# Up projections of a gated feed-forward by seven block products for eight, with the down projection in three groups

## What is computed

```
def conv_ffn(h, w_up, conv_w, conv_b, w_down):
    u = causal_dwconv(h @ w_up, conv_w) + conv_b
    gate, up = jnp.split(u, 2, axis=-1)
    return (jax.nn.silu(gate) * up) @ w_down
...
x = x + conv_ffn(rmsnorm(x, ffn_norm[layer]), ...)
```

## Time and profile before

| | |
|---|---|
| median of 3 runs | 2572.43 us (2566.87 to 2572.94) |
| the profiled execution | 2572.35 us, span of the core 2570.6 us |
| PE busy | 2326.0 us, 90% of the span |
| PEld, the weight loads (beside PE) | 1163.4 us, 45% |
| DVE, ACT, POOL busy | 1097.3, 692.2, 889.6 us (43, 27, 35%) |
| share of the chain that ended last, PE | 40% |
| granted PE clock, mean | 0.929 of full |

### The profile page before, as it was taken

How to read it: one execution, slowest core, us unless ns; L and a number is a source line. 1 busy time by engine, 2 the same in 40 slices (tenths; PEclk the granted TensorE clock), 3 DMA queues, 4 the chain that set the end, 5 groups by cost and what they waited for, 6 DMA issues and landing times. The chain is left out here.

```text
span 2570.6 us, 32294 instructions
## 1 busy us (share of the span) xinstructions
PE 2326.0 (90%) x12070; PEld 1163.4 (45%) x12070; DVE 1097.3 (43%) x1585; ACT 692.2 (27%) x989; POOL 889.6 (35%) x671
## 2 busy tenths in 40 slices
PE   5877657888999999999987989899899999999998
PEld 3433325644444444444443444885444444444444
DVE  7678888835433333321140043953453333331001
ACT  5245556612323222200021213311132222220000
POOL 6002304223434433444348022312343344334432
PEclk7888879999999999999998999558999999999999
DMA  4001100001111111111123001000111111111112
GB/s 148 17 1 33 39 11 1 18 25 41 50 49 49 49 53 53 47 54 45 53 61 98 0 26 33 9 1 17 49 34 56 49 49 49 50 56 45 51 53 80
DMA packets 185946, 109.32 MB, mean 43 GB/s; under 512 B 3871, under 2 KB 180422, under 8 KB 185878
## 3 DMA queue, kind: packets, MB, share of 16 engines
q1 hardware_dynamic: 185414, 107.00, 13.9%
q0 software_dynamic: 464, 1.39, 0.2%
HBM read 104.18 MB, written 4.19 MB: 42 GB/s over the span
## 5 line engine op out<-in xcount | busy, mean ns | idle before, releaser
L503 POOL TENSOR_SCALAR w_scaled<-stage 128x1024 f32<-128x1024 f32 (+1 forms) x184 | 189.7, 1031 | 1351.4 <-PE ps L699 1328.6
L699 PE MATMUL ps<-h_hi,w_hi 128*128 128x512 f16 x1696 | 511.1, 383 | 70.7 <-ACT work L1168 40.7
L699 PE MATMUL ps<-h_lo,w_hi 128*128 128x512 f16 x1696 | 510.3, 383 | 0.0
L699 PE MATMUL ps<-h_hi,w_lo 128*128 128x512 f16 x1696 | 509.8, 382 | 0.0
L699 PE MATMUL ps<-arena,w_hi 128*128 128x512 f16 x1920 | 494.9, 380 | 2.9 <-DVE small L1765 2.6
L1782 DVE SCALAR_TENSOR_TENSOR work<-ps,fvec,work 128x1023 f32<-128x1023 f32 (+1 forms) x176 | 225.5, 1282 | 509.0 <-ACT work L1233 496.1
L506 POOL TENSOR_TENSOR w_lo<-w_scaled,w_hi 128x1024 f16<-128x1024 f32 (+1 forms) x176 | 369.2, 2098 | 14.7
L699 PEld LDWEIGHTS ps<-arena,w_hi 128*128 128x128 f16 x1920 | 188.2, 98 | 231.6 <-issue 6.7
L699 PEld LDWEIGHTS ps<-h_hi,w_hi 128*128 128x128 f16 x1696 | 166.2, 99 | 276.9 <-issue 82.6
L699 PE MATMUL ps<-arena,w_lo 128*128 128x512 f16 x960 | 286.4, 380 | 0.0
L699 PEld LDWEIGHTS ps<-h_lo,w_hi 128*128 128x128 f16 x1696 | 167.5, 99 | 204.8 <-issue 8.0
(11 more groups left out here) (302 smaller groups left out, 2364.0 us busy)
## 6 DMA issues: line engine op xcount, KB each, us to landing
stage<-in_ffn_w_up_dram SPq DMA_DIRECT2D x88, 512.0 KB, 3.8
stage<-in_ffn_w_down_dram SPq DMA_DIRECT2D x32, 512.0 KB, 3.6
stage<-in_od_w_in_dram SPq DMA_DIRECT2D x20, 512.0 KB, 3.7
stage<-in_ev_w_in_dram SPq DMA_DIRECT2D x12, 512.0 KB, 3.6
stage<-in_ffn_w_down_dram SPq DMA_DIRECT2D x16, 384.0 KB, 3.2
arena<-in_x_dram SPq DMA_DIRECT2D x8, 512.0 KB, 6.3
stage<-in_ev_w_out_dram SPq DMA_DIRECT2D x8, 512.0 KB, 3.6
stage<-in_od_w_out_dram SPq DMA_DIRECT2D x8, 512.0 KB, 3.6
```

What stands on the lines that cost most here:

```text
L503: nc.gpsimd.tensor_scalar(scaled, src, W_SCALE, 1.0, ALU.mult, ALU.mult).then_inc(w_parts, 1)
L699: last = mm(out2[:, hf * HALF:(hf + 1) * HALF], w, a[:, k0 + k, hf * HALF:(hf + 1) * HALF], start=(first and k == 0 and pss == 0), stop=(l ...
```

## The change

In the 20 hidden tiles f = 2 to 21 of each layer, the gate and the up unit are computed together. The weights of the pair are seen as a 2x2 block matrix (gate and up by the two halves of the 1024 input channels), the activations as another (halves of the channels by halves of the positions). Eight block products of 12 matmuls make 96; here there are seven products, by sums of the weight blocks and of the activation blocks, and sums of the products: 84 matmuls.

- **POOL** no longer scales (L503) or rounds (L504) up weights. It makes four sums of 512-column blocks (`su_sums`) and the low parts of all seven blocks (`su_lows`), eight TENSOR_TENSOR instructions a pair.
- **ACT** scales both stage buffers in place (`su_scale`, 2048 elements), makes the high parts of seven blocks (`su_hi_raw`, `su_hi_sums`), and copies product P1 out of PSUM (`keep_p1`). The feed-forward on ACT, DVE and POOL is written out without loops.
- **DVE** makes four sums of activation blocks after the norm (2048 elements each), and five sums a pair (`cross`, 512 elements with one operand in PSUM) that PE and the convolution wait for.
- **PE** keeps the products of one f in four banks x, z, y, w, and waits inside a pair for DVE's sums: P7 for U2, P4 for U3, P3 for C22.
- **SP** loads both weight tiles of f+1 when POOL has read those of f (`su_read`): there is one `stage` for both, so a pair is not loaded while the one before it is still read.
- **f = 1** is computed plainly (96 matmuls), but from the new weight buffers, whose high part ACT makes ahead of its 16 norm tiles and whose low part POOL makes ahead of its norm tiles.
- **Memory.** The sums need room, so the hidden tiles are a ring of eight: groups of 8, 8 and 6 hidden tiles, each followed by its own down projection over all eight m, added to the residual: 24 residual additions a layer in place of 8. The first matmuls of a down projection wait for the last hidden tiles of the group.
- Outside the feed-forward, the **indexer** starts at block 2.

The core of the diff:

```diff
+            def su_sums(layer, f):
+                pool.wait_ge(su_scaled, X0 + su_of(layer, f) + 1)
...
+                if j:
+                    pool.wait_ge(su_split, j)
+                    pool.wait_ge(su_hi, hi_count(layer, f - 1) if f > 2 else hi_count(0, FT - 1))
+                G.tensor_tensor(sums_a[:, 0, :], up[:, 0, :], up[:, 1, :], ALU.add).then_inc(su_sum, 1)
+                G.tensor_tensor(sums_a[:, 1, :], gate[:, 0, :], up[:, 0, :], ALU.subtract).then_inc(su_sum, 1)
...
+            def ffn_split(layer):
+                split_section(f"up{layer}", 2, 1, peeled=2)
+                su_lows(layer, 1)
+                norm_lows(1 + 2 * layer)
+                su_sums(layer, 2)
+                su_lows(layer, 2)
+                for i, op in enumerate((1, 0, 2)):
+                    top_low(layer, i + 1, op)
+                su_sums(layer, 3)
+                top_low(layer, 4, 3)
+                su_lows(layer, 3)
+                for g, (f0, nf) in enumerate(GROUPS):
+                    for f in range(max(f0, 4), f0 + nf):
+                        su_sums(layer, f)
+                        su_lows(layer, f)
+                    pool.wait_ge(su_split, cross_of(layer, f0 + nf - 1) + 1)
+                    split_section(f"down{layer}{'abc'[g]}", 2, 4, lambda u: nf * P)
...
+                def crossed(f, i):
...
+                    pe.wait_ge(conv_done, i * 4 + (c0 + 2 * set_user(f) + 2))
...
+                    pe.wait_ge(su_split, i * 2 + (j + 1))
+                    product(x, A11, s, b_of(h_hi, 0, 0), b_of(h_lo, 0, 0), True)
...
+                    product(y, S2, s, *tops[1], True)
...
+                    product(z, S1, s, *tops[0], True)
...
+                    pe.wait_ge(cross_step, i * 10 + (5 * j + U2))
+                    product(y, S3, s, *tops[2], False)
+                    pe.wait_ge(p1_copied, i * 2 + (X0 + j + 1))
+                    product(x, A12, s, b_of(h_hi, 1, 0), b_of(h_lo, 1, 0), False)
...
+                    pe.wait_ge(cross_step, i * 10 + (5 * j + U3))
+                    product(y, A22, s, b_of(h_hi, 0, 1), b_of(h_lo, 0, 1), False)
+                    pe.wait_ge(cross_step, i * 10 + (5 * j + C22))
+                    product(z, S4, s, b_of(h_hi, 1, 1), b_of(h_lo, 1, 1), False)
...
+                if n % 2:
+                    su_scale(n // 2, 1)
+                    su_hi_raw(n // 2, 1)
                 for m in range(2 * KT):
                     hf, k = divmod(m, KT)
+                    if n % 2 and m == 12:
+                        su_scale(n // 2, 2)
...
+                    for f in range(max(f0, 2), f0 + nf):
+                        cross(f, U2)
+                        if f > f0:
+                            hidden(f - 1)
+                        cross(f, U3)
+                        cross(f, C22)
+                        if f > f0:
+                            hidden_low(f - 1)
+                        cross(f, C21)
+                        cross(f, C12)
+                        conv(f)
...
-            for b in range(NB):
+            for b in range(2, NB):
```

391 lines of the change are left out of this document (298 added, 93 removed).

## The result

The changed kernel takes 2529.85 us (median of 4 runs, 2521.63 to 2534.58); the kernel before, run beside it, 2569.65 (4 runs, 2566.8 to 2572.94). The ratio is 0.9844, 95% interval 0.9818 to 0.987: 1.6% faster, where 0.8% was forecast (2552). The sign was right, and the time lies in the range, at the number of rival A. The gain was twice the forecast.

What follows compares the result with a forecast made beforehand. PE, busy 90% of the span, was taken to bound the kernel. Removing 119.3 us and adding 49.1 a layer (98.2) gave net -21.1 from 2572.4, 2551.3, said as 2552 us; range 2528 to 2586.

Steps and rivals of the forecast that it cites:

- rival A: Feed-forward start mostly covered: costs 5 to 14 us for 20, short waits cost no clock; 2530 us; chance 0.13.
- Removed, 119.3 us: Time taken away: 103.6 us of matmuls, 12.1 of waits and low clock at the third unit, 3.6 of indexer blocks.
- The start: Start of each feed-forward: second norm tile 4.2 us later, then PE waits taken as 20 us, range 0 to 28.
- the walk: Start followed through POOL, ACT and DVE: POOL's lows of f = 3 ready at 709.8; PE stalls 18.5 us in all.
- The last stall: PE before P7 of f = 3: 2.6 us, as tap 2 of f = 2 stands on ACT behind a scale.
- ends of groups: Down projection's last k waits for the last hidden tile, 11.3 us after P3: 2.2 + 2.2 + 4.8 = 9.2 us a layer.
- Starts of groups: Next group's weights wait for the last down split: 4.5 us before P1, 0.6 before P7, twice a layer: 10.2 us.
- Clock behind these places: Clock falls after three waits a layer of 4.5 to 4.8 us: 3 x 2.05 less 0.6, 5.5 us.
- the clock behind waits of 2.2 to 2.9 us: PE's clock after these shorter waits: 0 to 2.8 us lost each, taken as 0.
- B: P7's wait for U2 in steady pairs: 0.6 us of room, sums come 1.0 later, 14 us lost; 2566 us; chance 0.15.
- C: The weight ring (load, scale, sums, lows) sets the steady pair's pace at 19.0 us, costing 31 us; 2583 us; chance 0.17.
- D: Clock falls inside the pairs, as PE waits on seven semaphores a pair: 72 us, 2624 us; chance 0.03.

Runs made afterwards that it cites:

- x_norm: Changed kernel with POOL making the first norm low part ahead of the weights' low parts of f = 1: 2533.48 us.
- x_nw: Changed kernel with matmuls without a use on PE in front of each feed-forward's norm, 80 small and 8 of 512 columns: 2527.63 us.
- x_pw: x_pre with 20 matmuls without a use on PE before P7 of f = 2: 2509.49 us.
- x_en: x_early with the edit of x_norm added: 2516.48 us.
- x_early: Changed kernel with the high parts of the weights' sums of f = 2 moved ahead on ACT, before an activation's high part and two tap 2: 2524.42 us.
- x_tops: Changed kernel with DVE's four activation sums at a layer's start cut to 16 columns of each block: 2517.24 us.
- x_pre: Changed kernel with the first pair's weights of the second and third group loaded, scaled and split ahead of the down weights: 2502.24 us, ratio 0.9747 to the kernel before.
- x_order: Changed kernel with DVE's hidden low part of tile 0 moved behind the subtraction U2 of f = 2: 2534.82 us.

## Why the gain was twice the forecast

Removed, 119.3 us: right but for the indexer. The 103.6 us of matmuls are confirmed by the 20.72 us pairs. Of the 3.6 us 0.8 was seen at the residual, inside a scatter of 3 us: **2.8 less** than forecast. Forecast for the feed-forwards alone was 115.7 - 98.2 = 17.5 us; measured 37.0. So what the change adds was put at 49.1 us a layer, and that was too much.

**The start was the failing step**: second tile 4.2 and waits 20, 24.2 us a layer. By my own walk PE without waits would have come to P7 of f = 3 at 697.5, 82.4 us after the residual (655.0, 675.8 and 693.9 of the walk, each less the 4.2, plus three products). It came 714.45 - 614.31 = 100.1 after it, in layer 1 98.9. **The start costs 17.8 and 16.5 us, not 24.2.** Of the low clock all that lies ahead of this is in it. In PE's rows 9.2 us of it are waits before L857 (7.0 in layer 1), where I had announced about 20, at three places and not six; the rest is mostly the second tile, 4.1 us later after the residual than before the change, and matmuls at the lower clock.

Adding the two terms was no double count, since the walk's waits are counted from a PE that is already 4.2 late. But they are not two costs that could be saved one by one. x_norm, x_nw and x_pw made PE earlier or faster ahead of P7 of f = 2, and it came 77.1 to 77.4 us after the residual, as in the changed kernel (77.2 and 77.0); x_en did so on top of x_early, and it stayed at x_early's 74.0. There is one cost, the lateness at the end of the chain, and that is what the walk had wrong.

**Where the walk was long.** It has POOL's lows of f = 3, for which PE waits at that tile's first product, ready at 709.8, 94.7 us after the residual. They ended at 704.0, 89.7 after it. Of these 5.0 us 2.0 lie ahead of POOL's last norm low (I had 649.8, it was 646.95): the 1.9 us for the scale of f = 2 cost nothing there. Behind it I had 60.0 us and it took 57.05. POOL's waits for ACT came to 5.1 us and not 9: the one for the sums' high parts was there, the one at the sums of f = 3 was not. The exclusions by DVE's four sums were 6.1 and not 8.5. Against that about 3.4 us came up that I had not counted, mostly POOL instructions that took 0.45 to 1.0 us longer beside other work of DVE.

The last stall, before P7 of f = 3, came as walked, from tap 2 behind a scale that waits for a load, in layer 0 2.37 us for 2.6 and in layer 1 0.65. Then I put 1.5 on top, from 18.5 to "I take 20", with bounds of 0 and 28: nothing but caution pointed up. So the wait of POOL for ACT is the main term that was mis-sized, 5.1 for 9, then the exclusion, 6.1 for 8.5, and by x_tops the chain hung not on what POOL lost by exclusion, but on DVE's first three sums and the 3.4 us for which POOL held them.

Smaller terms, a layer: ends of groups 1.44 + 1.44 + 4.02 = 6.9, forecast 9.2. From P3 the last hidden tile took 10.7 us and not 11.3 (the convolution 5.10 for 5.33, hand-overs the rest) and PE's cover was 9.2 and not 9.06, so the step was right and the size off by 0.8 at each. Starts of groups 8.1 and 8.7, forecast 10.2: the waits were 4.1 for 4.5, and the 0.6 before the next P7 did not come, as far as can be told because of the 1.2 us of room. Clock behind these places: 1.8 a start by x_pre, 1.5 and 2.5 at the last end (in windows of 2 us, busy time by what the clock lacked of 1.00): 5.1 and 6.1, forecast 5.5.

One term I had put at nothing, the clock behind waits of 2.2 to 2.9 us. In layer 0 four products follow P7 of f = 3 and its wait of 2.37 us without a pause, and take 12.1 us where in layer 1, behind 0.65 us, they take 10.3; the clock over them:

```profile
714.45:726.55 12.10, 12.10 (x49) 5.19 (x50) 5.90 (x5) 4.61 (x4) 9.49 (x7) 0.86 0.31 87
```

That is 1.7 us. At this place PE waited 2.1 to 2.6 us in twelve feed-forwards of the kernels with whole pairs of seven products, and behind nine of them the same 1.7 us are lost, behind three nothing. x_order's +3.0 us in layer 1 are for the most part this: its P7 of f = 3 comes 1.0 us later, after a wait of 2.3, and the four products behind it take 1.7 longer.

Added in all: 17.8 + 6.9 + 8.1 + 5.1 + 1.7 = 39.6 in layer 0, 16.5 + 6.9 + 8.7 + 6.1 = 38.2 in layer 1, for 49.1 each. The removed side is 51.8 us of matmuls a layer and the third unit's 5.3 and 6.8. That makes the feed-forwards 57.1 - 39.6 = 17.5 and 58.6 - 38.2 = 20.4 us shorter, measured 17.1 and 19.9.

**The rivals.** A gave 2530 for a start of 5 to 14 us, the second tile's 4.2 not counted; the time is A's, the reason is half so. In A's terms the start cost 13.6 and 12.3, at the upper end, and POOL's lost time did run into its wait for ACT, though DVE's sums lay on the chain. Short waits did lose clock, and 8.2 us of what I had put too high were at the ends and starts of groups. B and C named real limits with too little room given them: 1.2 us for B's 0.6, and a ring of 16.05 for C's 19.0. D: none; the window over four pairs shows 1.00. On the rule of the Trainium skill (SBUF — State Buffer, "Who interferes with whom"), that a DVE instruction with two SBUF inputs and a POOL instruction that reads SBUF shut each other out for a whole instruction, the trace now agrees from POOL's side too: 2.05 us on each of three instructions, where the rows before had shown 0.4 us for a short instruction. My 2.1 at the start was right by size, the count of four was not.

**The chances.** 0.13 was too little for A. The start, its exclusions, the ends and the starts of groups were all put on the high side, and such errors add.

## What to carry to other kernels

At a seam where the bottleneck engine waits for others, compute one time, that at which it can go on, by the longest chain from a fixed mark, and subtract when it would have arrived. Don't add up its delays along the way: what lies ahead of the last wait is covered. To find that chain, make the bottleneck engine earlier and see whether the mark moves; then look on the other engines for a queue in which something ready stands behind something that waits, as the weights' high parts did here behind an activation's. And measure the room of a tight wait by adding work to it, since three cheap instructions tell it to a tenth of a us.
